# A decoder layer with product-key experts on one core: output projections split over the attention heads, expert picks turned earlier, one-hots built four tokens at a time with the gates applied by ScalarE

## The chip, the cores and the metric

One Trainium2 chip, one core, everything in float32. The metric is the device time of one launch in microseconds. The kernel is written by engine: TensorE (PE), VectorE (DVE), ScalarE (ACT), GpSimd (POOL) and SyncE (SP) each have one ordered list of instructions, tied together by counting semaphores. A matrix product in float32 shows as two entries each of weight load and matmul in the profile.

## What is computed

512 tokens (4 blocks of 128) of width 1024 go through one layer:

```
h   = x @ w_in                                   # 7 column groups of 512
r   = swish(g) * GroupNorm(retention(rot(q), rot(k), v))       # 4 heads
d   = RMSNorm((softmax(q1 k1') - lam softmax(q2 k2')) v) * 0.8 # 4 heads
x   = LayerNorm(alpha x + concat(r, d) @ w_out)
s   = (x @ w_query) . sub_keys                   # 8 heads, 2 halves, 128 keys
      top 16 of each half, top 16 of the 256 sums -> 128 experts per token
gate= softmax(best scores)
y   = sum_e gate_e * gelu(x . u_e) * v_e         # of 16384 experts
out = LayerNorm(alpha x + y)
```

## The kernel before, in words

**Two ways to the experts.** Blocks 0 and 3 are *gathered*: for each of 128 picks per token a row of 128 x 1024 is fetched by an indirect DMA (POOL, L443) into a ring of 8, `ring`; first 128 rows of u for `dot` (L1052), then 128 of v for `add_row` (L1070). That makes 512 rows, taken in a fixed order by `rows(n)`, which VectorE calls wherever its list has room. The running count is `taken[0]`. POOL issues the next gather when VectorE has used the row 8 before it. Blocks 1 and 2 are *dense*: for each of 128 expert blocks n, `up(n)` (L730) multiplies x with the block of uT, `hidden(n)` (L966) takes the Gelu, `mask_hidden(n)` (L1335) multiplies with the gates G, and `add(n, d)` (L760) sums h times the block of V in PSUM. `up(n)` may run two blocks ahead of `hidden`. Up to NH = 56 hidden blocks are kept before the main loop starts.

**The gates G** come from picks. `norm_picks(d)` (L1313) normalises their gates after ScalarE's Exp in `take_picks(d)` (L977), TensorE turns the three columns (first key, second key, gate) in `turn_picks(d)` (L740), ScalarE copies them to `pT`. `hot_quads(d)` (L1322) builds for each token two one-hots of 128, `b_hot` and `a_hot`, the second already times the gate; `quad(q)` (L749) multiplies those of four tokens, `take_quad(q)` (L985) copies the result to a stage, and every 8 quads ScalarE spills a stage of 2 MB to the buffer gd in HBM. `load_g` (L364) brings it back by expert. There are 32 quads for each of the two dense blocks d; the rings are 4 one-hot slots and 5 PSUM banks.

**Order of the work.** (1) Block 0 goes through projections, attention, output and query alone. (2) `project_1` does the projections of blocks 1 to 3 with retention between them; VectorE takes 2 rows before each rotary and 4 before each swish gate. (3) For b = 1 to 3: `attend(b)` runs four heads. For each the score of the next head, two Exps with row sums on ScalarE (`attention`, L891), `softmax_join` on VectorE, transposes, a copy and the product with v; VectorE takes 2 rows per head. `diff_norm(b)` (L1224) follows, then `mixed_out(b)` (L661): transposes, copies by ScalarE, and both halves of the output projection (`out_half`, L682) into banks W 2 and 3, in which attention also works. `attend(b+1)` waits until `ln1(b)` (L1235) has read them. (4) `query` for three blocks, with scores copied to SBUF; VectorE retrieves block 1 (`retrieve`, L1246: best_keys, best_pairs, best_experts for two heads at a time). (5) TensorE does 40 expert blocks (UP_FIRST), then picks and quads of d = 0 with one `up` per four quads, then those of d = 1. In ScalarE's list `take_picks(0)` stands behind `hidden(39)`. VectorE's list has best_keys(2, 0), norm_picks(0), the rest of that retrieve, hot_quads(0), three retrieves with three rows each, norm_picks(1), the rest of 128 dots, hot_quads(1), weigh(0). (6) The main loop of 128 steps n: TensorE `add(n)` for both d and `up(n + 56)`, VectorE `mask_hidden(n + 8)`, in the early steps the four retrieves of block 3, and 4 rows a step up to 384 rows, later 3 a step from n = 66 on, where `weigh(1)` stands. `gathered_gelu` (L958) on ScalarE waits for the last 8 dots of its block. (7) The last sums and norms.

SP loads in list order: weights as slots come free (`load_w`; the query's first weights wait for the first half of block 3's output projection), uT into 4 slots, V into 4 slots (each block when `add` has freed one), G in groups of 8.

Two orders that a sentence tells badly, VectorE's and ScalarE's lists in stage 5:

```
best_keys(2, 0); norm_picks(0); best_pairs(); best_experts(2, 0)
hot_quads(0)                                   # VectorE
for s in range(1, 4): retrieve(2, s); rows(3)
norm_picks(1); rows(E - taken[0]); hot_quads(1); weigh(0)

for n in range(UP_FIRST): hidden(n)            # ScalarE
for d in range(ND):
    take_picks(d)
    for q in range(d * QUADS, (d + 1) * QUADS):
        take_quad(q)
        if q % 4 == 3: hidden(UP_FIRST + q // 4)
gathered_gelu(0)
```

## Time and profile before

| | |
|---|---|
| median of 3 runs | 1799.67 us (1797.59 to 1803.29) |
| the profiled execution | 1803.09 us, its span 1801.0 us |
| TensorE busy | 1457.8 us (81%), mean granted clock 0.901 |
| VectorE busy | 1201.1 us (67%) |
| ScalarE busy | 174.5 us (10%) |
| GpSimd busy (issuing gathers) | 598.8 us (33%) |
| moved by DMA | 503.05 MB, mean 279 GB/s |

Busy shares are means over stages with different limits, so the table says little by itself. A group of instructions is named by its line, its engine, and what it writes and reads. A granted clock of 1.00 is TensorE's full 2.4 GHz, 0.50 the lower level of 1.2 GHz. A window's row gives, for a stretch of the span, busy time of each engine with its count in brackets (PE, PEld, DVE, ACT, POOL), then PE's granted clock, the busy share of the DMA engines and GB/s. The chain that ended last is followed back from the last instruction; each of its rows is a stretch in which that work held the end.

### The profile page before, as it was taken

Reading aid. Unit: us, or ns where it says so; the run is one execution under the profiler, and the core shown is the slowest. Engines: PE = TensorE matmul, PEld = TensorE weight load, DVE = VectorE, ACT = ScalarE, POOL = GpSimd, SP = SyncE. Lnnn points to the kernel's source line nnn. Section 1 sums busy time; section 2 is a strip of 40 time slices with the busy share of each in tenths; the row PEclk is TensorE's granted clock in tenths of the full one; section 3 lists DMA queues with packets and bytes.
Section 4 is the critical chain, followed back from the end, with each engine's and each line's share of the span. In section 5 each row is a group of like instructions: output and inputs, shape, how many; then the busy total and the mean of one; then the engine's idle time right before and its main releaser. Section 6 shows DMA issues by size and latency. Waiting matters only on the chain.

```text
span 1801.0 us, 15732 instructions
## 1 busy us (share of the span) xinstructions
PE 1457.8 (81%) x5374; PEld 937.7 (52%) x5374; DVE 1201.1 (67%) x2884; ACT 174.5 (10%) x400; POOL 598.8 (33%) x517
## 2 busy tenths in 40 slices
PE   7889998665799997930589999998988957888776
PEld 5474464333457886830475666555655535333232
DVE  2367865668478102998977998666666669776773
ACT  1110001122011111310230001000000000000000
POOL 0005131224411000004303446455455557654620
PEclk9989999666899999975698999999999978999888
DMA  9938464334933543444769999999999999999973
GB/s 344 362 130 308 174 217 147 122 117 128 354 129 101 187 153 117 152 164 157 286 222 364 365 365 359 409 405 405 408 406 404 406 408 378 405 406 405 405 294 105
DMA packets 161950, 503.05 MB, mean 279 GB/s; under 512 B 15056, under 2 KB 33744, under 8 KB 160720
## 3 DMA queue, kind: packets, MB, share of 16 engines
q0 software_dynamic: 73728, 268.47, 39.4%
q1 hardware_dynamic: 86992, 216.81, 32.7%
q10 hardware_dynamic: 1152, 16.78, 2.5%
q8 instruction: 43, 0.70, 0.2%
q14 instruction: 35, 0.29, 0.0%
HBM read 483.13 MB, written 18.87 MB: 279 GB/s over the span
## 4 chain that ended last, share of the span: by engine, by line
PE 35%; DVE 24%; DMA 24%; POOL 7%; issue 6%; SPq 1%; ACT 1%; DVEq 0%; POOLq 0%
DMA arena<-uv,idx 21%; PE X L736 9%; POOL arena L443 7%; PE W L716 6%; PE W L483 6%; DVE xs L1070 5%; DVE arena L1052 3%; PE W L763 3%; PE W L688 2%; PE W L489 2%; DVE lng L1331 2%; PE W L756 1%; DVE arena L1330 1%; DMA arena<-uv 1%; DMA arena<-w_in 1%
## 5 line engine op out<-in xcount | busy, mean ns | idle before, releaser
L443 POOL DMA_INDIRECT arena<-uv,idx x512 | 598.4, 1169 | 1126.3 <-DVE arena L1052 632.2
L736 PE MATMUL X<-arena 128*128 128x256 f32 x2048 | 458.6, 380 | 27.0 <-ACT arena L975 26.3
L736 PEld LDWEIGHTS X<-arena 128*128 128x128 f32 x2048 | 389.1, 191 | 111.6 <-issue 61.9
L763 PE MATMUL W<-arena 128*128 128x512 f32 x768 | 363.2, 625 | 62.9 <-DMA arena<-uv 52.8
L1070 DVE SCALAR_TENSOR_TENSOR xs<-arena,gate,xs 128x1024 f32<-128x1024 f32 x256 | 328.7, 1284 | 110.9 <-DMA arena<-uv,idx 98.3
L1052 DVE SCALAR_TENSOR_TENSOR arena<-arena,xs 128x1024 f32<-128x1024 f32 x256 | 306.7, 1223 | 95.5 <-DMA arena<-uv,idx 92.7
L763 PEld LDWEIGHTS W<-arena 128*128 128x128 f32 x768 | 152.6, 201 | 240.8 <-issue 205.1
L483 PE MATMUL W<-arena 128*128 128x512 f32 x320 | 143.7, 605 | 9.6 <-DMA arena<-w_in 8.9
L716 PE MATMUL W<-arena 128*128 128x128 f32 (+1 forms) x512 | 117.1, 392 | 1.4 <-ACT arena L926 1.4
L1331 DVE TENSOR_SCALAR lng<-iota_f,both_uses 128x128 f32<-128x128 f32 x256 | 106.6, 431 | 0.0
L483 PEld LDWEIGHTS W<-arena 128*128 128x128 f32 x320 | 60.8, 194 | 81.7 <-issue 77.0
L716 PEld LDWEIGHTS W<-arena 128*128 128x128 f32 x512 | 80.4, 199 | 36.3 <-issue 2.4
L756 PE MATMUL W<-lng,arena 128*128 128x128 f32 x416 | 56.6, 292 | 52.4 <-issue 40.3
L1330 DVE TENSOR_SCALAR arena<-iota_f,both_uses 128x128 f32<-128x128 f32 x256 | 94.5, 370 | 0.0
L975 ACT ACTIVATE arena<-X 128x256 f32<-128x256 f32 x96 | 36.5, 383 | 499.9 <-PE X L736 470.8
L756 PEld LDWEIGHTS W<-lng,arena 128*128 128x128 f32 x416 | 53.6, 203 | 55.3 <-issue 40.7
L763 PE MATMUL W<-arena,kT 128*128 128x512 f32 x128 | 63.1, 644 | 21.7 <-DMA arena<-uv 14.2
L1317 DVE TENSOR_REDUCE gsum<-both_uses 128x8 f32<-128x128 f32 x2 | 0.6, 284 | 118.3 <-ACT both_uses L980 118.3
L763 PE MATMUL W<-arena,rv 128*128 128x512 f32 x128 | 58.4, 608 | 14.8 <-DMA arena<-uv 11.9
L489 PE MATMUL W<-arena 128*128 128x128 f32 (+1 forms) x256 | 59.1, 389 | 5.2 <-DVE arena L1145 3.7
L763 PEld LDWEIGHTS W<-arena,kT 128*128 128x128 f32 x128 | 25.8, 206 | 54.6 <-issue 39.5
L489 PEld LDWEIGHTS W<-arena 128*128 128x128 f32 x256 | 39.1, 194 | 22.8 <-issue 6.3
(185 smaller groups left out, 971.3 us busy)
## 6 DMA issues: line engine op xcount, KB each, us to landing
arena<-uT SPq DMA_DIRECT2D x128, 512.0 KB
arena<-uv SPq DMA_DIRECT2D x128, 512.0 KB
arena<-w_in SPq DMA_DIRECT2D x13, 2048.0 KB, 13.0
arena<-peer_w_query SPq DMA_DIRECT2D x8, 2048.0 KB, 12.0
gd<-arena ACTq DMA_DIRECT2D x8, 2048.0 KB, 7.2
arena<-gd SPq DMA_DIRECT2D x16, 1024.0 KB
arena<-w_out SPq DMA_DIRECT2D x4, 2048.0 KB, 14.0
arena<-uv,idx POOLq DMA_INDIRECT x512
```

What stands on the lines that cost most here:

```text
L443: pool.indirect_dma_start(out=ring[:, s % RING, :], out_offset=None, in_=rows, in_offset=bass.IndirectOffsetOnAxis(ap=idx[:, col:col + 1], ...
L483: last = nc.tensor.matmul(bank, actT[:, k, part * P:(part + 1) * P], wts[slot][:, k, :], start=(k == 0), stop=(k == KD - 1))
L489: last = nc.tensor.matmul(bank[:, at:at + n_tok], wts[slot][:, k, h * P:(h + 1) * P], actT[:, k, toks], start=(k == 0), stop=(k == KD - 1))
L716: last = nc.tensor.matmul(dst, wts[slot][:, k, i * P:(i + 1) * P], actT[:, k, toks], start=(k == 0), stop=(k == KD - 1))
L736: last = nc.tensor.matmul(h_bank(n), u_ring[n % UR][:, k, :], actT[:, k, P:P + TD], start=(k == 0), stop=(k == KD - 1))
L756: last = nc.tensor.matmul(bank[:, m * P:(m + 1) * P], b_hot[:, q % OH_RING, m, :], a_hot[:, q % OH_RING, m, :], start=True, stop=True)
L763: last = nc.tensor.matmul(sum_banks(d)[:, half, :], h_slot(n)[:, d * P:(d + 1) * P], v_ring[n % VR][:, half * HW:(half + 1) * HW], start=( ...
L975: nc.scalar.activation(h_slot(n), h_bank(n), ACT.Gelu).then_inc(h_ready, 1)
L1052: STT(out=ring[:, r, :], in0=ring[:, r, :], scalar=1.0, in1=xs[:, GATHERED[g], :], op0=ALU.mult, op1=ALU.mult, accum_out=hid[:, col:col + ...
L1070: STT(out=xs[:, b, :], in0=ring[:, r, :], scalar=gate[:, g * E + e:g * E + e + 1], in1=xs[:, b, :], op0=ALU.mult, op1=ALU.add).then_inc(ro ...
L1330: TS(b_hot[:, q % OH_RING, m, :], iota_f[:], pT[d % 2][:, 1, t:t + 1], None, ALU.is_equal)
L1331: last = TS(a_hot[:, q % OH_RING, m, :], iota_f[:], pT[d % 2][:, 0, t:t + 1], pT[d % 2][:, 2, t:t + 1], ALU.is_equal, ALU.mult)
```

## The change

1. *Output projection.* The halves of block b's projection no longer follow `attend(b)` but stand between the heads of `attend(b + 1)`: the turn of the mixed rows beside head 0, one half beside head 1, one beside head 2, and `turn_x1(1)` beside head 3 of block 3. They use the PSUM tensors X and ACC, not W. Scores of the next block's first head are made beside the last head. VectorE's `ln1(b - 1)` moves from behind head 0 to the end of block b.
2. *Picks.* `UP_FIRST` goes; 6 expert blocks stand before the first `turn_picks`, 18 before the second, and one `up` follows every second quad. `gathered_gelu(0)` moves between the two sets of quads, `weigh(0)` in front of `hot_quads(1)`.
3. *One-hots.* One comparison of 128 x 512 for each of `b_hot` and `a_hot` instead of four of 128 x 128; `a_hot` without the gate. ScalarE scales it in place, four Copies of 128 x 128 with a column of `pT` as the scale (`gate_hot`), one quad ahead of the quad's copy.
4. *Rows.* Taken 3 and 5 in the projections (2 and 4), 2 before each retention norm (1), 1 per head (2), 6 and 24 around ln1(3) (8 and 12), 4 per retrieve of block 1 (3), 1 per two quads (0), none per retrieve of block 2 (3). By the start of the main loop 144 rows are taken instead of 128, `weigh(1)` stands at n = 62 instead of 66.

```diff
 GT = 8
-UP_FIRST = NH - ND * QUADS // 4
+UP_BEFORE = [6, 18]
+FIRST_V3 = 62
...
-        def out_banks(ph):
+        def mix_bank(b, half):
-            return [W[:, 2 * ph + half, :] for half in range(2)]
+            return X[:, half * HW:(half + 1) * HW] if b else W[:, half, :]
+        x1_bank = mix_bank
+        def out_of(b):
+            return ACC[:] if b else W[:, 2:4, :].rearrange("p a n -> p (a n)")
...
                 keys_n = (b + 1) * P
-                if h:
-                    pe.wait_ge(exps_ready, H * b + h)
-                elif b > 1:
-                    pe.wait_ge(mix_taken, 2 * b)
-                else:
+                if b == 1 and h == 0:
                     pe.wait_ge(proj_taken_act, takes(fill[0], "act"))
+                else:
+                    pe.wait_ge(exps_ready, H * b + h)
                 for c in range(2):
...
                         score(b, h + 1)
+                    elif b < NB - 1:
+                        score(b + 1, 0)
+                    beside(b, h)
                     n = H * b + h
                     pe.wait_ge(a_ready, n + 1)
-                    if b == 1 and h == 0:
-                        pe.wait_ge(ret_normed, NB)
-                    elif h == 0:
-                        pe.wait_ge(out_read, b)
+                    if h == 0:
+                        if b == 1:
+                            pe.wait_ge(ret_normed, NB)
+                        pe.wait_ge(mix_ready, b)
                     else:
...
-            def mixed_out(b):
+            def beside(b, h):
-                turn_mixed(b)
-                if b > 1:
-                    turn_x1(b - 1, out_banks(1))
-                if b < NB - 1:
-                    score(b + 1, 0)
-                if b > 1:
-                    pe.wait_ge(x1_taken, 2 * b)
-                for half in range(2):
-                    out_half(b, half)
+                if b > 1 and h == 0:
+                    turn_mixed(b - 1)
+                elif b > 1 and h < 3:
+                    out_half(b - 1, h - 1)
+                elif b == 3 and h == 3:
+                    turn_x1(1)
...
                 pe.wait_ge(mix_ready, b + 1)
+                if b == 3:
+                    pe.wait_ge(x1_taken, 4)
                 for half in range(2):
...
                         src = swish[:, b - 1, :] if half == 0 else work[:, HW:2 * HW]
-                        last = nc.tensor.transpose(W[:, half, k * P:(k + 1) * P], src[:, k * P:(k + 1) * P], ident[:])
+                        last = nc.tensor.transpose(mix_bank(b, half)[:, k * P:(k + 1) * P], src[:, k * P:(k + 1) * P],
+                                                   ident[:])
                     last.then_inc(mix_turned, 1)
...
                 pe.wait_ge(mix_taken, 2 * (b + 1))
+                if b > 1:
+                    pe.wait_ge(out_read, b)
                 slot, count = wslot(1, WIN + half)
...
                 for k in range(KD):
-                    last = nc.tensor.matmul(W[:, 2 + half, :], mixT[:, k, :], wts[slot][:, k, :],
+                    last = nc.tensor.matmul(ACC[:, half * HW:(half + 1) * HW], mixT[:, k, :], wts[slot][:, k, :],
                                             start=(k == 0), stop=(k == KD - 1))
...
                 attend(b)
-                mixed_out(b)
-            turn_x1(3, out_banks(0))
+            turn_mixed(3)
+            out_half(3, 0)
+            out_half(3, 1)
+            turn_x1(2)
+            turn_x1(3)
             query(1, WAVES[1])
             pe.wait_ge(scores_stored, 4 + 3 * WQ)
-            for n in range(UP_FIRST):
-                up(n)
+            n = 0
             for d in range(ND):
+                for _ in range(UP_BEFORE[d]):
+                    up(n)
+                    n += 1
                 turn_picks(d)
...
                     quad(q)
-                    if q % 4 == 3:
-                        up(UP_FIRST + q // 4)
+                    if q % 2:
+                        up(n)
+                        n += 1
             pe.wait_ge(quad_taken, ND * QUADS)
...
                     act.wait_ge(a_turned, n)
+                    if h == 0:
+                        act.wait_ge(squares_ready, b)
                     for c in range(2):
...
                     last.then_inc(exps_ready, 1)
+                    beside(b, h)
                     act.wait_ge(a_turned, n + 1)
...
+            def beside(b, h):
+                if b > 1 and h == 0:
+                    take_mixed(b - 1)
+                elif b == 3 and h == 3:
+                    take_x1(1)
             def take_mixed(b):
...
+            def gate_hot(q):
+                d, t = q // QUADS, 4 * (q % QUADS)
+                act.wait_ge(hot_found, q + 1)
+                for m in range(4):
+                    last = nc.scalar.activation(a_hot[:, q % OH_RING, m, :], a_hot[:, q % OH_RING, m, :], ACT.Copy,
+                                                scale=pT[d][:, 2, t + m:t + m + 1])
+                last.then_inc(hot_ready, 1)
             def take_quad(q):
...
                 attention(b)
-                take_mixed(b)
-                if b > 1:
-                    take_x1(b - 1, out_banks(1))
-            take_x1(3, out_banks(0))
+            take_mixed(3)
+            take_x1(2)
+            take_x1(3)
             query(1, WAVES[1])
-            for n in range(UP_FIRST):
-                hidden(n)
+            n = 0
             for d in range(ND):
+                for _ in range(UP_BEFORE[d]):
+                    hidden(n)
+                    n += 1
                 take_picks(d)
+                act.wait_ge(pT_ready, d + 1)
+                gate_hot(d * QUADS)
                 for q in range(d * QUADS, (d + 1) * QUADS):
+                    if q + 1 < (d + 1) * QUADS:
+                        gate_hot(q + 1)
                     take_quad(q)
-                    if q % 4 == 3:
-                        hidden(UP_FIRST + q // 4)
-            gathered_gelu(0)
+                    if q % 2:
+                        hidden(n)
+                        n += 1
+                if d == 0:
+                    gathered_gelu(0)
             for n in range(NH, NT):
...
                     gate_exp(1)
-                elif n == NH + 64:
+                elif n == NH + FIRST_V3 - 2:
                     gathered_gelu(1)
...
                 dve.wait_ge(mixer_ready, 2 * (b + 1))
-                src = W[:, 2:4, :].rearrange("p a n -> p (a n)")
-                STT(out=xs[:, b, :], in0=xs[:, b, :], scalar=ALPHA, in1=src, op0=ALU.mult,
+                STT(out=xs[:, b, :], in0=xs[:, b, :], scalar=ALPHA, in1=out_of(b), op0=ALU.mult,
                     op1=ALU.add).then_inc(out_read, 1)
...
                    op=ALU.mult).then_inc(pk_ready, 1)
+                dve.wait_ge(pk_ready, d + 1)
...
                         dve.wait_ge(quad_ready, q - OH_RING + 1)
-                    for m in range(4):
-                        t = 4 * (q % QUADS) + m
-                        TS(b_hot[:, q % OH_RING, m, :], iota_f[:], pT[d % 2][:, 1, t:t + 1], None, ALU.is_equal)
-                        last = TS(a_hot[:, q % OH_RING, m, :], iota_f[:], pT[d % 2][:, 0, t:t + 1],
-                                  pT[d % 2][:, 2, t:t + 1], ALU.is_equal, ALU.mult)
-                    last.then_inc(hot_ready, 1)
+                    t = 4 * (q % QUADS)
+                    TT(out=b_hot[:, q % OH_RING, :, :], in0=iota_f[:].unsqueeze(1).to_broadcast([P, 4, P]),
+                       in1=pT[d % 2][:, 1, t:t + 4].unsqueeze(2).to_broadcast([P, 4, P]), op=ALU.is_equal)
+                    TT(out=a_hot[:, q % OH_RING, :, :], in0=iota_f[:].unsqueeze(1).to_broadcast([P, 4, P]),
+                       in1=pT[d % 2][:, 0, t:t + 4].unsqueeze(2).to_broadcast([P, 4, P]),
+                       op=ALU.is_equal).then_inc(hot_found, 1)
+                    if q % 2:
+                        rows(1)
...
                 if FILLS[n][1] == RG:
-                    rows(4)
+                    rows(5)
                     swish_gate(n)
                 else:
-                    rows(2)
+                    rows(3)
                     rotary(n)
...
                         rows(1)
-                rows(1)
+                rows(2)
                 retention_norm(b)
...
                         softmax_max(b, h)
-                    rows(2)
+                    rows(1)
                     softmax_join(b, h)
-                    if b > 1 and h == 0:
-                        ln1(b - 1)
-                rows(2)
-                diff_norm(b)
                 if b < NB - 1:
                     softmax_max(b + 1, 0)
-            rows(8)
+                if b > 1:
+                    ln1(b - 1)
+                else:
+                    rows(2)
+                diff_norm(b)
+            rows(6)
             ln1(3)
-            rows(12)
+            rows(24)
             for s in range(4):
                 retrieve(1, s)
-                rows(3)
+                rows(4)
             best_keys(2, 0)
...
                 retrieve(2, s)
-                rows(3)
-            norm_picks(1)
             rows(E - taken[0])
-            hot_quads(1)
+            norm_picks(1)
             weigh(0)
+            hot_quads(1)
             for n in range(LEAD):
...
                         best_experts(3, s)
-                if taken[0] == 3 * E and n < 66:
-                    pass
-                else:
-                    if n == 66:
-                        weigh(1)
-                    rows(min(4, 3 * E - taken[0]) if n < 66 else 3)
+                if n == FIRST_V3:
+                    weigh(1)
+                rows(min(4, 3 * E - taken[0]) if n < FIRST_V3 else 3)
                 if n == 40:
```

Left out are new semaphore names, the matching changes of the copies on ScalarE (`take_mixed`, `take_x1` with the new banks) and the calls of `turn_x1` without a bank argument.

## Rows read from the trace of the kernel before

**Rows 1.** Windows of the kernel: busy us (x count) per engine, clock, DMA share, GB/s.

```profile
305.00:468.00 163.00, 97.78 (x301) 52.98 (x300) 113.36 (x267) 31.83 (x98) 52.42 (x39) 0.70 0.48 158
362.00:380.00 18.00, 10.13 (x33) 6.12 (x34) 17.37 (x36) 5.17 (x15) 8.86 (x7) 0.50 0.51 156
778.00:875.00 97.00, 5.79 (x30) 4.49 (x29) 86.90 (x253) 3.73 (x7) 40.92 (x34) 0.55 0.55 189
959.00:1107.00 148.00, 148.00 (x514) 97.23 (x513) 140.37 (x322) 11.19 (x25) 72.40 (x58) 1.00 0.96 357
1107.00:1495.00 388.00, 330.16 (x1081) 209.23 (x1079) 263.19 (x388) 16.48 (x43) 212.50 (x194) 0.93 1.03 405
```

**Rows 2.** The chain that ended last: start us, us, what.

```profile
224.99 4.58 DVE arena L1052 x8
...
338.21 14.99 PE W L688 x32
...
391.21 14.09 PE W L688 x32
...
468.26 23.45 PE W L716 x64
...
568.65 138.41 PE X L736 x640
...
930.45 3.80 PE W L756 x32
...
1729.49 39.72 PE W L763 x88
```

**Rows 3.** The waits: engine and line waited for, total us, times, longest.

```profile
DVE gsum L1317 <- ACT both_uses L980: 118.3, 1, 118.3
```

**Rows 4.** DMA issues on the page: line, count, KB each.

```profile
arena<-uv SPq DMA_DIRECT2D x128, 512.0 KB
```

**Rows 5.** Timeline of the attention blocks, 353 to 386 us, all engines.

```profile
353.29 1.22 DVE L1240 SCALAR_TENSOR_TENSOR xs<-xs,W 128x1024 f32<-128x1024 f32 x1 [9.43 <-PE W L688]
...
359.74 1.28 DVE L1103 SCALAR_TENSOR_TENSOR xs<-xs,lnr,lng 128x1024 f32<-128x1024 f32 x1
...
366.60 0.90 PE L653 MATMUL W<-ident,arena 128*128 128x128 f32 x3 [1.06 <-DVE arena L1203]
...
369.65 1.65 PE L635 MATMUL W<-dkT,arena 64*128 64x384 f32 x4
...
381.96 0.17 DVE L1228 TENSOR_SCALAR rstd<-ssq 128x4 f32<-128x4 f32 x1 [2.10 <-ACT arena L910]
...
384.35 1.13 DVE L1231 SCALAR_TENSOR_TENSOR arena<-W,rstd,both_uses 128x128 f32<-128x128 f32 x4
```

**Rows 6.** Timeline of DVE from 560 to 820 us.

```profile
566.78 0.87 DVE L1257 MAX8 best_v<-rv 128x8 f32<-128x128 f32 x4 [5.21 <-ACT rv L949]
...
720.24 0.28 DVE L1330 TENSOR_SCALAR arena<-iota_f,both_uses 128x128 f32<-128x128 f32 x1
...
777.69 0.53 DVE L1331 TENSOR_SCALAR lng<-iota_f,both_uses 128x128 f32<-128x128 f32 x1
...
797.05 0.87 DVE L1257 MAX8 best_v<-kT 128x8 f32<-128x128 f32 x4
...
812.54 1.22 DVE L1052 SCALAR_TENSOR_TENSOR arena<-arena,xs 128x1024 f32<-128x1024 f32 x1
```

**Rows 7.** Groups of instructions by form: busy us, mean ns, idle before.

```profile
L1297 DVE TENSOR_TENSOR cand<-pos_f,iota_f 128x512 f32<-128x512 f32 x32 | 22.3, 697 | 1.1
...
L975 ACT ACTIVATE arena<-X 128x256 f32<-128x256 f32 x96 | 36.5, 383 | 499.9 <-PE X L736 470.8 <-issue 29.1
...
L991 ACT ACTIVATE arena<-W 128x512 f32<-128x512 f32 x52 | 31.0, 597 | 77.4 <-PE W L756 77.4
...
L975 ACT ACT_TABLE_LOAD x4 | 5.1, 1283 | 0.1
...
L871 ACT ACTIVATE arena<-X,nmax 128x128 f32<-128x128 f32 x8 | 2.8, 376 | 9.0 <-DVE nmax L1212 9.0
```

25 lines of the change are left out of this document (14 added, 11 removed).

## The prediction

> **What bounds the kernel now.** I read the windows first, stage by stage, then the waits, the chain that ended last, and the two timelines where a stage is neither full of matrix work nor of transfers. The last 850 us are held by transfers: from 1107 us until the gathers end the DMA engines are busy all the time, at 405 GB/s up to 1495 us [rows 1]. Between 959 and 1107 us TensorE (148 of 148 us) and VectorE (140) are full too, at 357 GB/s. Only the tail is TensorE's: 88 matrix entries in 39.7 us, 0.451 us each, and one step n has 8 of them, so 3.6 us a step [rows 2].
>
> Before that the engines take turns. For 118.3 us VectorE stands in front of norm_picks(0), because ScalarE takes the Exp of the picks only after 40 expert blocks [rows 3], and the 40 blocks are 138.4 us of TensorE, 3.46 us each [rows 2]. Then VectorE alone works from 778 to 875 us (86.9 of 97 us) with TensorE at 5.8 us [rows 1]. In attention neither is full: 97.8 and 113.4 of 163 us [rows 1]; TensorE does both halves of an output projection in 14.99 and 14.09 us [rows 2] in front of the next block's transposes.
>
> So two things decide the end: when the main loop can start, and how many rows of 512 KB [rows 4] are still to be gathered by then.
>
> **Projections.** Nine rows more are taken there. A row is 4.58/4 = 1.15 us of VectorE [rows 2]. VectorE has slack except in front of the second and third swish gate, where the row of the chain at 225 us stands; one of the added rows lies on it: **+1.2 us**. The others are covered by VectorE's waits for TensorE, and would cost 1.15 us each without them (bounds 0 and 10).
>
> **Attention** now takes 163 us [rows 1]. I walk it with the present durations. A row fewer per head and one fewer at the end of block 1 leave the first block 23.0 instead of 27.3 us. In block 2 head 0 needs a row, a join and the maxima and Exp of head 1: 5.8 us. Heads 1 and 2 each hold half a projection, 7.0 us (half of 14.09 [rows 2]), between the score of the next head and the transposes. From transposes to the next score it is 369.65 - 366.60 = 3.05 us, the score is 1.65 [rows 5]: 11.6 us a head, where VectorE has nothing to hide the half with, since its next maxima and join hang on the Exp behind it. Then join, the maxima of block 3 (4.4), ln1 of block 1 (353.29 to 361.02, 7.7) and the norm (381.96 to 385.48, 3.5, with its mark 3.6) [rows 5]: 5.8+23.2+4.4+7.7+3.6 = 44.7. Block 3 has longer rows: 6.5+2 x 12.7+1.9+7.7+3.6 = 45.1, with turn_x1(1) beside it. Last come transposes and copies (2.7), both halves of block 3 (14.0), ln1 (7.7), transposes and copies (2.7): 27.1. Sum 23.0+44.7+45.1+27.1 = 139.9 from the first maxima at 306.5, so the query would start at 446.4 instead of 468: -21.6 us. SP's queue: the query's first weights, 2 MB, wait for the first half of block 3 and then have 17 us, at 0.405 MB/us 5.2 us alone, so they stay hidden; so do POOL's gathers, eight deep in the ring. **The clock** takes something back. In the heads the granted clock is 0.50, the lower level of 1.2 GHz [rows 1], and of the present projections the first, after a longer stretch of such work, took 0.9 us more than the second (14.99 and 14.09 [rows 2]). Four halves will start behind small work where two pairs did; I take 0.5 us each, near that row: **-19.5 us**. Bounds: -25 (no such cost, and copies that overlap) and -8 (0.9 us at each of six pieces, and 8 us of joins that come late). The Trainium skill, "TensorE: Matmul & The Clock Gate", section on the HAM clock gate, says that the array gets every pulse only after it was kept busy and half of them after idling. By that rule, applied to each half, the part would be rival (b); the trace has both levels, 0.50 here and 1.00 in the early main loop [rows 1], and no row of halves that stand alone.
>
> **From the query to the first one-hot.** The query itself is unchanged, 568.65 - 468.26 = 100.4 us [rows 2], and starts at 468.3+1.2-19.5 = 450.0; the first block of uT at 550.4, the sixth ends at 571.2. VectorE's 24 rows after ln1(3) run into the loads of the query's weights; four more of them would still be covered, as block 1's last scores come 566.78 - 468.26 = 98.5 us into the query [rows 6], at 548.5. From there retrieve 812.54 - 797.05 = 15.5 us, four rows 4.6, and best_keys to best_experts with norm_picks between them 16.4: 585.0. One-hots are two 128x512 comparisons; the nearest row is L1297, a comparison with both inputs broadcast, 0.697 us [rows 7]. That is 1.3 us a quad against 57.9/32 = 1.8 now (720.24 to 778.2) [rows 6]. First matmul of a quad at about 587.6. TensorE, that had been at it until 709 us, idles 16 us here.
>
> **A set of 32 quads** is now 57.9 us, bound by VectorE. After the change TensorE has 16 blocks between the 32 quads. Four quads are 3.80 us [rows 2], so two are 1.8 and with the block 3.46+1.8 = 5.26 us a pair. VectorE needs 2 x 1.3+1.15 = 3.8 and is no bound. ScalarE has eight scalings, two quad copies of 0.60 and one Gelu of 0.38 [rows 7]. A scaling of 128x128 by a column: 0.376 us is the nearest row, an Exp with such an operand (L871); plain forms take 0.383 for 256 columns and 0.597 for 512, so by their slope 0.276 for 128 [rows 7]. Four in a row are 1.1 to 1.5 us, and I take 1.3. Sum 2.6+1.2+0.4 = 4.2: no bound either. But it is in order: behind an odd quad ScalarE waits for the block, does Gelu (0.38), and only then scales the second next quad (1.3), while TensorE has one quad ready (0.9). **Added wait:** 0.8 us a pair, bounds 0.3 and 1.1; behind it queue the quad and the block after it. A pair is 6.04, a set 96.6 us, 1.5 us more for the cold start: 587.6 to 685.7.
>
> **Between the sets.** VectorE is free some 9 us before, at 677, and does three retrieves (46.5) and the last nine dots (10.3): 733.8. gathered_gelu(0) stands in ScalarE's queue in front of hidden(22), so TensorE gets two blocks ahead and then waits for that very moment. The 18 blocks of UP_BEFORE thus do not run beside VectorE: 16 x 3.46 = 55.4 us, and 2.5 for the clock, end at 792.5, with VectorE waiting, as in [rows 3], for the Exp (table load 1.28 [rows 7], 1.9 in all). Norm (0.9), weigh(0) (some 2.1, five short instructions) and the first one-hot and scaling (2.6) give 800.0. The second set ends at 897.1 with its block (0.5 for the clock), its last quad at 893.6; now that is 930.45+3.80 = 934.2 [rows 2]. **The main loop starts 40.6 us earlier**; less the 18.3 of the two parts above, **22.3 us** come from here (bounds 10 and 38, by the two ends of the wait and 4 us of DVE's lead).
>
> **Main loop.** 144 rows instead of 128 are taken by then, so the first two thirds take 60 steps, not 64, and gathers end at step 104, not 108. Before that point 16 gathers and 4 blocks of V fewer must land: 20 x 0.524 MB at 0.405 MB/us [rows 1, 4] is -25.9 us. But the four steps are then in TensorE's tail, 4 x 3.6 = +14.4 [rows 2]. Sum: **-11.5 us**. Bounds -5 and -20 (the early steps, which TensorE and VectorE fill, give nothing back or everything).
>
> **Sum.** +1.2 - 19.5 - 22.3 - 11.5 = -52.1 against 1803.1 us for the profiled execution (span 1801.0): 1751.0. That execution lies 3.4 us above the median of the three runs, 1799.7, from which the same sum gives 1747.6. I say 1748. The measurement can tell about 0.3%, 5.4 us, from nothing.
>
> **Rivals.**
> (a) *The wait in the quads is hidden and the halves cost less*: ScalarE at its lower prices leaves 0.3 us a pair (-16), attention gives its 25 (-5): 1727. For it, ScalarE's 4.2 of 5.3 us; against it, its order.
> (b) *Half clock in attention*: all six halves at 1.2 GHz, 14 us instead of 7: +42, 1790. For it the 0.50 among the heads, against it the 14.09 us of a present pair, behind heads at 0.50 [rows 1, 2].
> (c) *The early rows return nothing*, since TensorE (148 of 148) and not DMA sets the early main loop: 1760.
> (d) *Table loads, slower than before*: each pair has a scaled copy behind a Gelu. If the scaled form needs another table, that is two loads of 1.28 us a pair on the in-order wait, 32 x 2.56 = 82 us: 1830. It decides from 52/32 = 1.6 us a pair. Against it: plain copies and Gelus alternate now with 4 loads in all [rows 7].
> (e) *The early turn does not come about*, VectorE waits for something else in the first set as long as now: the middle gives 0, 1770.
>
> **Chances.** Forecast 0.62, (a) 0.11, (b) 0.05, (c) 0.10, (d) 0.03, (e) 0.09. The forecast alone spans 1735 to 1762. The range reaches to (a) and (e), 1726 to 1770. Slower is 0.04, (d) and 0.01 for (b) with the bad ends of the other bounds; within 0.3% 0.02, from (b) too; faster 0.94.
>
> **What would show it.** In the waits, VectorE's 118 us gone and a wait of some 55 to 60 us in front of the second norm_picks; TensorE idle some 16 us before the first quad and 40 us behind the 24th block; the last quad at 894 us; a quad pair at 6.0 us; query at 450; the last gathered row added 66 us earlier than now, with 17 steps of tail behind it. The step that is weakest is the attention walk: half projections of 7 us at 1.00 confirm it, 14 us refute it. Wrong would also be a first set shorter than 85 us, or a main loop whose DMA share falls below 1.0 after its first 150 us.

## The result, and the profile after

| | before | after |
|---|---|---|
| median (range), 4 runs each | 1800.89 us (1797.59 to 1803.29) | 1741.39 us (1738.73 to 1744.23) |
| profiled execution, its span | 1803.09, 1801.0 us | 1741.73, 1739.7 us |
| VectorE busy | 1201.1 us | 1163.3 us |
| ScalarE busy | 174.5 us | 241.9 us |

The ratio is 0.9671, with a 95% interval of 0.9648 to 0.9694. The changed kernel takes 61.3 us less by the spans of the two profiled executions (59.5 by the medians), where the prediction's sum was 52.1. Below, "the set" is the 32 quads of one dense block, and "a block" of TensorE is one expert block of `up`, 16 matrix entries.

The stages come out of four marks on the chain: the first attention score (305.73 before, 309.34 after), the query's first matmul, the last spill of the second set (`gd<-arena`, the eighth of eight), and the end. The third mark of the kernel before:

```profile
934.90 7.15 DMA gd<-arena
```

| stretch | before | after | change | forecast |
|---|---|---|---|---|
| start to first attention score | 305.7 | 309.3 | +3.6 | +1.2 |
| attention, to the query | 162.5 | 135.6 | -27.0 | -19.5 |
| query to the last spill | 466.6 | 447.5 | -19.2 | -22.3 |
| last spill to the end | 866.1 | 847.3 | -18.8 | -11.5 |

The chain that ended last, after; start us, us, what:

```profile
226.28 5.72 DVE arena L1097 x10
232.75 8.25 PE W L497 x16
...
340.18 7.44 PE ACC L699 x16
350.58 7.06 PE ACC L699 x16
382.38 7.06 PE ACC L699 x16
...
418.04 16.38 PE ACC L699 x32
444.89 23.51 PE W L729 x64
...
582.62 3.78 PE W L769 x16
...
716.76 10.32 DVE arena L1097 x18
727.83 58.28 PE X L749 x256
793.71 3.78 PE W L769 x16
...
892.35 7.13 DMA gd<-arena
```

The pairs of halves of 14.99 and 14.09 us [rows 2] are now four separate halves; the pair of block 3 is still a pair. The query has come forward from 468.26 to 444.89. The 640 entries in one piece in front of the quads [rows 2] are gone, and in their place stand 256 entries at 727.83, behind the last dots.

The waits of after; engine and line waited for, total us, times, longest:

```profile
PE X L749 <- ACT arena L1004: 67.2, 2, 37.1
...
DVE gsum L1361 <- ACT both_uses L1009: 61.1, 1, 61.1
```

VectorE's 118.3 us [rows 3] have become 61.1 in front of the other norm_picks. ScalarE's timeline has the Gelu of the gathered block, `gathered_gelu(0)`, with its wait in brackets:

```profile
727.10 0.31 ACT L993 ACTIVATE hid<-hid 128x128 f32<-128x128 f32 x1 [42.89 <-DVE arena L1097]
```

The three waits lock one another: ScalarE waits 42.9 us for the last dots, TensorE 37.1 for ScalarE to take the Gelu of block 22, and then VectorE 61.1 for ScalarE to come to the Exp behind the blocks.

Windows of after (columns as in rows 1): the first set, the dots without blocks, the blocks without dots, and most of the main loop:

```profile
583.00:676.00 93.00, 82.58 (x474) 73.83 (x474) 61.67 (x125) 55.78 (x164) 15.37 (x16) 0.98 0.69 237
676.00:728.00 52.00, 14.13 (x73) 12.20 (x72) 49.25 (x166) 3.86 (x11) 8.58 (x5) 0.69 0.35 113
728.00:792.00 64.00, 58.65 (x259) 50.64 (x259) 3.56 (x10) 8.23 (x19) 3.75 (x4) 0.95 0.52 180
...
1069.00:1430.00 361.00, 301.83 (x987) 192.09 (x986) 246.06 (x380) 15.84 (x42) 198.95 (x181) 0.92 1.03 405
```

Read the second and third together. VectorE is busy 49.25 of 52 us while TensorE has 14.13, and then TensorE 58.65 of 64 us while VectorE has 3.56. Those are two pieces of work that need nothing of each other, one behind the other. In the first set no engine is full: TensorE 82.58 of 93 us, VectorE 61.67, ScalarE 55.78. The main loop is bound by transfers as before, 405 GB/s [rows 1].

One pair of quads on the chain inside the first set:

```profile
599.10 3.47 PE X L749 x16
...
602.59 0.38 ACT arena L1004
602.97 1.17 ACT lng L1019 x4
...
604.19 1.16 PE W L769 x8
605.35 3.47 PE X L749 x16
```

From one block to the next it is 6.25 us. TensorE ends the block, ScalarE takes its Gelu, then scales the next quad, and only then has TensorE something to do. The scaling, and the table loads on the line of that Gelu (busy us, mean ns, idle before):

```profile
L1019 ACT ACTIVATE lng<-lng,both_uses 128x128 f32<-128x128 f32 x256 | 80.9, 391 | 12.4 <-DVE lng L1376 12.4
...
L1004 ACT ACT_TABLE_LOAD x4 | 5.1, 1283 | 0.1
```

Table loads have stayed at 4 on the line of the blocks' Gelu, as in [rows 7], and the scalings' own line has none. The new comparison of 128 x 512 takes VectorE 690 ns.

### The profile page after: what moved, and what is told of

It is laid out like the page before. It is cut to its first block, busy times and chain, and to the rows that moved or that the text cites. A ratio compares the mean times of both kernels' runs of the same rounds, so it can differ in the third digit from the quotient of the medians.

```text
span 1739.7 us, 15609 instructions
## 1 busy us (share of the span) xinstructions
PE 1458.6 (84%) x5374; PEld 936.8 (54%) x5374; DVE 1163.3 (67%) x2500; ACT 241.9 (14%) x656; POOL 589.1 (34%) x517
## 3 DMA queue, kind: packets, MB, share of 16 engines
q0 software_dynamic: 73728, 268.47, 41.3%
## 4 chain that ended last, share of the span: by engine, by line
PE 46%; DVE 21%; DMA 20%; POOL 4%; ACT 4%; issue 3%; SPq 2%; DVEq 0%; ACTq 0%
DMA arena<-uv,idx 13%; PE X L749 11%; PE W L776 11%; PE W L729 7%; PE W L491 6%; DMA arena<-uv 5%; POOL arena L451 4%; DVE xs L1115 4%; DVE arena L1097 3%; PE ACC L699 3%; PE W L497 2%; ACT lng L1019 2%; PE W L769 2%; DMA arena<-w_in 1%; PE W L739 1%
## 5 line engine op out<-in xcount | busy, mean ns | idle before, releaser
L451 POOL DMA_INDIRECT arena<-uv,idx x512 | 588.6, 1150 | 1064.5 <-DVE arena L1097 490.7
L749 PE MATMUL X<-arena 128*128 128x256 f32 x2048 | 465.3, 382 | 67.9 <-ACT arena L1004 67.2
L776 PE MATMUL W<-arena 128*128 128x512 f32 x768 | 356.1, 615 | 51.1 <-DMA arena<-uv 39.5
L491 PE MATMUL W<-arena 128*128 128x512 f32 x320 | 144.0, 606 | 10.5 <-DMA arena<-w_in 9.8
L769 PE MATMUL W<-lng,arena 128*128 128x128 f32 x416 | 60.7, 293 | 34.0 <-ACT lng L1019 34.0
L1374 DVE TENSOR_TENSOR arena<-iota_f,both_uses 128x512 f32<-128x512 f32 x64 | 44.2, 690 | 61.9 <-PE W L769 48.9
L1019 ACT ACTIVATE lng<-lng,both_uses 128x128 f32<-128x128 f32 x256 | 80.9, 391 | 12.4 <-DVE lng L1376 12.4
L769 PEld LDWEIGHTS W<-lng,arena 128*128 128x128 f32 x416 | 55.4, 202 | 40.5 <-ACT lng L1019 39.2
L1389 DVE TENSOR_TENSOR arena<-arena 128x256 f32<-128x256 f32 x96 | 38.3, 418 | 30.1 <-DMA arena<-gd 30.1
```

The lines of the kernel that those rows point to most:

```text
L451: pool.indirect_dma_start(out=ring[:, s % RING, :], out_offset=None, in_=rows, in_offset=bass.IndirectOffsetOnAxis(ap=idx[:, col:col + 1], ...
L491: last = nc.tensor.matmul(bank, actT[:, k, part * P:(part + 1) * P], wts[slot][:, k, :], start=(k == 0), stop=(k == KD - 1))
L749: last = nc.tensor.matmul(h_bank(n), u_ring[n % UR][:, k, :], actT[:, k, P:P + TD], start=(k == 0), stop=(k == KD - 1))
L769: last = nc.tensor.matmul(bank[:, m * P:(m + 1) * P], b_hot[:, q % OH_RING, m, :], a_hot[:, q % OH_RING, m, :], start=True, stop=True)
L776: last = nc.tensor.matmul(sum_banks(d)[:, half, :], h_slot(n)[:, d * P:(d + 1) * P], v_ring[n % VR][:, half * HW:(half + 1) * HW], start=( ...
L1019: last = nc.scalar.activation(a_hot[:, q % OH_RING, m, :], a_hot[:, q % OH_RING, m, :], ACT.Copy, scale=pT[d][:, 2, t + m:t + m + 1])
```

## The experiments

Twelve kernels. Those from the changed kernel first ask where its remaining loss sits and what its one-hots are worth (1 to 4), then what its parts gave (5, 6, and 12 from the kernel before), then how far the cure goes (7 to 11). The kernel before ran at 1801.5 to 1802.3 us beside them, and all ratios are against it.

| | kernel | us (range) | ratio, 95% interval |
|---|---|---|---|
| 1 | Gelu of the gathered block behind the 18 blocks | 1702.29 (1700.46 to 1703.86) | 0.9449 [0.9434, 0.9465] |
| 2 | 24 blocks first, none between the sets | 1744.31 (1741.74 to 1748.80) | 0.9683 [0.9661, 0.9705] |
| 3 | one-hots and gates on VectorE as before | 1713.23 (1711.35 to 1715.63) | 0.9512 [0.9496, 0.9527] |
| 4 | ScalarE scales one quad further ahead | 1713.57 (1713.18 to 1716.31) | 0.9514 [0.9498, 0.9530] |
| 5 | kernel before, with split projections alone | 1789.64 (1787.87 to 1791.44) | 0.9926 [0.9903, 0.9950] |
| 6 | no rows added in the second set | 1758.24 (1757.33 to 1761.77) | 0.9762 [0.9737, 0.9787] |
| 7 | 1 and 4 | 1672.01 (1670.60 to 1674.43) | 0.9281 [0.9257, 0.9304] |
| 8 | 7 with 10 blocks first | 1673.43 (1672.10 to 1676.27) | 0.9288 [0.9265, 0.9312] |
| 9 | 7 with 9 blocks first, norm later | 1665.10 (1661.12 to 1668.76) | 0.9241 [0.9217, 0.9265] |
| 10 | 9 with 8 more rows in the second set | 1658.41 (1654.32 to 1660.45) | 0.9201 [0.9178, 0.9225] |
| 11 | 1 and 3 | 1670.86 (1668.75 to 1672.62) | 0.9274 [0.9251, 0.9297] |
| 12 | kernel before, with early turn alone | 1752.22 (1746.12 to 1753.74) | 0.9719 [0.9694, 0.9744] |

### 1. The Gelu of the gathered block, behind the 18 blocks

```diff
@@ ScalarE's list, for d in range(ND)
                 for _ in range(UP_BEFORE[d]):
                     hidden(n)
                     n += 1
+                if d:
+                    gathered_gelu(0)
                 take_picks(d)
...
-                if d == 0:
-                    gathered_gelu(0)
```

> Changed kernel, with gathered_gelu(0) behind the 18 expert blocks in ScalarE's list instead of in front of them. Theory (two queues take turns): the 18 blocks now run while VectorE does its three retrieves and nine dots. They end 18 x 3.46 = 62 us after the first set of quads, at about 745 us instead of 786, and the second set starts at about 753 instead of 793.7: 41 us less, total 1741 - 41 = 1700 (1697 to 1706), and ScalarE's hold of TensorE (PE X waits for ACT, 37 us) is gone. Rival (the main loop is what counts, being held by DMA, and an earlier start is partly given back): the second set starts 41 us earlier but the total falls by 20 or less, 1720 or more.

39 us less than the changed kernel, and the second set starts at 753.35 instead of 793.71. The chain of this kernel:

```profile
679.89 65.63 PE X L749 x304
```

The blocks now follow the first set without a hole, beside VectorE's dots, and the wait in front of the second norm_picks has shrunk from 61.1 to

```profile
DVE gsum L1361 <- ACT both_uses L1009: 21.2, 1, 21.2
```

The edit moves one short ScalarE instruction past 18 blocks that don't need it, and nothing else.

### 2. All blocks in front of the first quads

```diff
-UP_BEFORE = [6, 18]
+UP_BEFORE = [24, 0]
```

> Changed kernel with UP_BEFORE = [24, 0] instead of [6, 18]: the picks of the first dense block turn 18 expert blocks later, none stand between the sets. Theory (the serial wait between the sets takes back what the early turn gives): first quad 62 us later, at about 644, first set ends about 744, VectorE's retrieves and dots at about 792, and the second set starts at once behind them, at about 799: 6 us later than now, total about 1747 (1742 to 1752). Rival (the early turn is what made the change faster): the 62 us are lost, 1795 or more.

1744.31 us, 3 more than the changed kernel, which the intervals of the two don't tell from nothing. The first quad is 60 us later (643.10 against 582.62), the second set starts at 794.87 against 793.71. VectorE waits the same 62 us, at the first norm_picks instead of the second:

```profile
DVE gsum L1361 <- ACT both_uses L1009: 63.9, 2, 61.9
```

With ScalarE's list as the change has it, turning the picks 18 blocks earlier thus gives almost nothing: 62 us of cover won in front are lost behind. The run doesn't undo the early turn as a whole, though: its first quad still comes 79 us before that of the kernel before (643.10 against 722.18), since 24 blocks stand in front instead of 40. A changed kernel with 40 in front was not run.

### 3. One-hots and gates on VectorE, as before

```diff
-                    TT(out=b_hot[:, q % OH_RING, :, :], in0=iota_f[:].unsqueeze(1).to_broadcast([P, 4, P]),
...
+                    for m in range(4):
+                        t = 4 * (q % QUADS) + m
+                        TS(b_hot[:, q % OH_RING, m, :], iota_f[:], pT[d % 2][:, 1, t:t + 1], None, ALU.is_equal)
+                        last = TS(a_hot[:, q % OH_RING, m, :], iota_f[:], pT[d % 2][:, 0, t:t + 1],
+                                  pT[d % 2][:, 2, t:t + 1], ALU.is_equal, ALU.mult)
+                    last.then_inc(hot_found, 1)
...
-                pe.wait_ge(hot_ready, q + 1)
+                pe.wait_ge(hot_found, q + 1)
```

The `gate_hot` calls of ScalarE's list are gone with it.

> Changed kernel with the one-hots of the kernel before: eight comparisons of 128x128 a quad on VectorE, the gate in the second one, and no scaling on ScalarE. Theory (a pair of quads is 6.25 us only because TensorE waits for ScalarE's scaling; its own work is 5.26): VectorE needs 8 x 0.45 + 1.15 = 4.8 us a pair, still less than TensorE, so a pair falls to 5.3 us, each set by 15 us, total about 1741 - 31 = 1710 (1706 to 1718). Rival (the cheaper one-hots are what made the sets fit): VectorE becomes the bound, a pair takes 6.2 us or more, total 1741 or more.

28 us less than the changed kernel. A window of its first set:

```profile
580.00:660.00 80.00, 80.00 (x482) 73.68 (x481) 78.19 (x305) 24.94 (x46) 15.56 (x16) 0.98 0.77 276
```

TensorE is full, 80.00 of 80 us, at 5.24 us a pair. VectorE is nearly so, 78.19 us, and that costs nothing. Added to the other parts, the third part of the change made the kernel slower by 28 us.

### 4. ScalarE scales a quad ahead

```diff
-                    if q + 1 < (d + 1) * QUADS:
+                    end = (d + 1) * QUADS
+                    if (q % 2 or q == d * QUADS) and q + 1 < end:
                         gate_hot(q + 1)
+                    if q % 2 and q + 2 < end:
+                        gate_hot(q + 2)
```

> Changed kernel, ScalarE scales one quad further ahead: behind an odd quad it scales the quad after the next before it waits for the expert block. Theory (the wait is one of order in ScalarE's list, not of its load of 4.5 us a pair): the waits of TensorE for the scaled rows vanish, a pair falls from 6.25 to 5.3 us, total about 1710 (1706 to 1716), the same as with the gates on VectorE. Rival (ScalarE is loaded too high and only the bound moves): a pair stays above 5.9 us, total 1733 or more.

1713.57 us. The chain inside its first set has no ScalarE left, only TensorE, 1.78 + 3.46 = 5.24 us a pair:

```profile
605.03 0.89 PE W L769 x8
605.92 0.89 PE ACC L769 x8
606.81 3.46 PE X L749 x16
```

The one-hots with ScalarE's scaling cost as much as those of VectorE alone, within 0.4 us, once the scaling doesn't stand behind the wait for a block. The 28 us were the order of ScalarE's list, not its work: the window 583 to 676 us has ScalarE at 60.14 us here and 55.78 in the changed kernel.

### 5. Split projections alone, from the kernel before

`attend` calls what stands beside each head, as in the change; picks, rows, quads and one-hots stay as before.

```diff
-            def mixed_out(b):
+            def beside(b, h):
-                turn_mixed(b)
-                if b > 1:
-                    turn_x1(b - 1, out_banks(1))
-                if b < NB - 1:
-                    score(b + 1, 0)
...
+                if b > 1 and h == 0:
+                    turn_mixed(b - 1)
+                elif b > 1 and h < 3:
+                    out_half(b - 1, h - 1)
+                elif b == 3 and h == 3:
+                    turn_x1(1)
```

> Kernel before with the attention part alone: halves of the projection between the heads of the next block, ln1 at the block's end, and everything else (rows taken, picks, one-hots, main loop) as before. In the changed kernel the stretch from the first attention score to the query's first matmul is 27 us shorter, but it also takes 16 rows fewer there. Theory (rows are exposed except beside a half): the 4 heads of block 1, heads 0 and 3 of blocks 2 and 3 and the rows at the ends of blocks 2 and 3 bring back some 12 rows of 1.15 us, so the split itself is worth 13 us: total about 1788 (1784 to 1792). Rival (the rows are hidden and the split does it all): 27 us, 1775 or less.

12.7 us less than the kernel before. The chain:

```profile
341.57 7.67 PE ACC L699 x16
...
425.62 16.92 PE ACC L699 x32
453.00 23.79 PE W L729 x64
```

From the first score (304.70) to the query it is 148.3 us, 14.2 less than before. The change has 135.6. In this stretch the two kernels differ only in the rows that VectorE takes, so the other 12.7 of the 27.0 come from those.

### 6. No rows added in the second set

```diff
-FIRST_V3 = 62
+FIRST_V3 = 66
...
-                    if q % 2:
+                    if q % 2 and d == 0:
```

> Changed kernel without the 16 added rows in the second set of quads, so that the main loop begins with 128 rows taken and weigh(1) stands at n = 66, as before. From the last quad on this is the kernel before. Theory (all of the main loop's gain is these 16 rows): the second set takes as long as now, and the total rises by the 18.8 us by which the stretch behind the last quad became shorter: about 1760 (1757 to 1763). Rival (my sum of 11.5 was right and 7 us came from elsewhere): 1753 or less.

17 us more than the changed kernel. The second set and its last spill keep their times (792.34 and 890.99, against 793.71 and 892.35), so all of it is main loop. VectorE's timeline of the kernel before at the first adds of the main loop and at `weigh(1)`:

```profile
957.78 2.68 DVE L1070 SCALAR_TENSOR_TENSOR xs<-arena,gate,xs 128x1024 f32<-128x1024 f32 x2
...
1499.21 2.71 DVE L1070 SCALAR_TENSOR_TENSOR xs<-arena,gate,xs 128x1024 f32<-128x1024 f32 x2
```

541.4 us between the two, and 541.5 in this run (912.70 to 1454.18). In the changed kernel, with the end of its last gathered row:

```profile
914.15 5.44 DVE L1115 SCALAR_TENSOR_TENSOR xs<-arena,gate,xs 128x1024 f32<-128x1024 f32 x4
...
1424.29 4.07 DVE L1115 SCALAR_TENSOR_TENSOR xs<-arena,gate,xs 128x1024 f32<-128x1024 f32 x3
...
1667.02 5.11 DVE L1389 TENSOR_TENSOR arena<-arena 128x256 f32<-128x256 f32 x15
```

510.1 us (914.15 to 1424.29). The 16 rows take four steps out of this phase: 16 gathers, 4 blocks of V and 4 of U, 24 x 0.524 MB at 0.405 MB/us = 31.1 us, and 31.3 are measured.

### 7. Both cures

The edits of 1 and 4 together.

> Changed kernel with gathered_gelu(0) behind the 18 blocks and ScalarE's scaling one quad further ahead, both together. Theory (TensorE is then the bound from the first quad to the last): the two gains of 39 and 28 us add up, since VectorE's dots (at about 712) still end before the 18 blocks (at about 730): total about 1674 (1670 to 1680). Rival (the faster sets only expose VectorE, or the main loop gives the start back): 1690 or more.

1672.01 us, 69.4 less than the changed kernel, against 39.1 + 27.8 = 66.9 for the two alone. The two losses sat in different stretches (the hole between the sets, the pairs within them), and so they add.

### 8. Ten blocks first

```diff
-UP_BEFORE = [6, 18]
+UP_BEFORE = [10, 14]
```

> The kernel with both mends and UP_BEFORE = [10, 14]: four of the blocks that stood between the sets go in front of the first picks, where TensorE idles some 14 us until VectorE has the first one-hot. Theory: the first quad is held by VectorE and stays where it is, the second set starts 14 us earlier; 1660 (1657 to 1665) if the kernel with both mends gives 1674. Rival (the Exp of the picks comes 14 us later in ScalarE's list and holds norm_picks and the first quad back by as much): no gain, within 3 us of that kernel.

No gain (1673.43). The theory was that TensorE idles in front of the first quad and could do four blocks there for nothing. The chain says that the idle time had moved, not gone:

```profile
545.20 34.81 PE X L749 x160
...
580.44 1.28 ACT L1009
...
596.01 3.78 PE W L769 x16
```

Ten blocks end at 580.0, the Exp stands behind their Gelus, and VectorE, which waits 13.6 us for it, still has best_pairs and best_experts to do: 14.3 us between the end of the Exp's table load (the piece of 1.28 us) and the first quad. Counted from the query's first matmul (444.74, in 7 442.64), the first quad is 13.6 us later than in 7, against 4 x 3.46 = 13.8 us of blocks won, and the second set starts after 293.6 us where 7 has 293.8. That is the rival.

### 9. Nine blocks first, and norm_picks(0) behind best_experts

```diff
-UP_BEFORE = [6, 18]
+UP_BEFORE = [9, 15]
...
-            norm_picks(0)
             best_pairs()
             best_experts(2, 0)
+            norm_picks(0)
```

> The kernel with both mends, UP_BEFORE = [9, 15], and norm_picks(0) moved behind best_experts(2, 0), so that the Exp of the picks may come 10 us later. With ten blocks first and norm_picks in its old place the first quad was 11 us later, because the Exp stands behind the blocks in ScalarE's list. Theory (that list is the whole cause): the Exp ends at about 579, when VectorE is ready for it, the first quad comes 2 us later than with six blocks, three blocks of 3.46 us are gone between the sets: 8 us less than the kernel with both mends, about 1664 (1661 to 1668). Rival (TensorE is the bound in any order, moving blocks gives nothing): within 3 us of 1672.

1665.10 us, 6.9 less than 7. The steps must be counted from the query, because this execution already starts it 4.2 us later, with nothing changed up to there. The query's first matmuls in 7 and in this run:

```profile
442.64 23.51 PE W L729 x64
```

```profile
446.86 23.66 PE W L729 x64
```

From there the first quad comes after 139.4 us (586.23), in 7 after 137.7 (580.36): 1.7 later, where 2 were expected. The second set comes after 286.1 us (732.92), in 7 after 293.8 (736.40): 7.7 earlier, where 8 were expected. So the theory holds in its steps too. (Its "11 us later" for ten blocks is 13.6 by the same count.)

### 10. More rows in the second set

```diff
-FIRST_V3 = 62
+FIRST_V3 = 60
...
-                    if q % 2:
+                    if q % 2 or d and q % 4 == 2:
```

> The kernel of e9_nine_first with 24 instead of 16 added rows in the second set of quads (three in four quads), 152 rows taken before the main loop, weigh(1) at n = 60. Theory (16 rows taken early are worth 17 us, and VectorE and the DMA engines still have room in the set, 9.4 us of work in 10.5 a four of quads and some 350 of 405 GB/s): 8 more rows give 8.5 us, about 1656 (1652 to 1660). Rival (the gathers no longer come in time and the set grows): 1662 or more.

1658.41 us, 6.7 less than 9, the fastest of all: 83 us below the changed kernel and 143 below the one before. Its window between the two sets:

```profile
669.00:728.00 59.00, 55.80 (x260) 48.69 (x258) 48.65 (x164) 8.57 (x20) 12.31 (x9) 1.00 0.69 238
```

Between the sets TensorE (55.80) and VectorE (48.65 of 59 us) now work side by side, where the changed kernel needs 52 + 64 us one after the other. The second set takes eight more rows and isn't longer (its last spill starts at 816.46, in 9 at 817.23), but the rows give 6.7 us where 8.5 were expected.

### 11. One-hots on VectorE, Gelu late

The edits of 1 and 3 together.

> Changed kernel with the one-hots of the kernel before (gates on VectorE) and gathered_gelu(0) behind the 18 blocks. Theory (cheaper one-hots are worth nothing while TensorE bounds the sets): the same 1672 to 1675 as with ScalarE's scaling ahead. Rival (VectorE, later free, now ends its dots behind the 18 blocks, and the cheaper one-hots begin to count): 1680 or more.

1670.86 us against 1672.01 for 7: the same within the intervals. With TensorE the bound of a pair, the new one-hots are worth nothing by time. What they leave is room on VectorE, which 10 uses for its eight rows; whether the old ones would have had that room beside 78.19 of 80 us was not run.

### 12. The early turn alone, from the kernel before

```diff
-UP_FIRST = NH - ND * QUADS // 4
+UP_BEFORE = [6, 34]
...
-            for n in range(UP_FIRST):
-                up(n)
+            n = 0
             for d in range(ND):
+                for _ in range(UP_BEFORE[d]):
+                    up(n)
+                    n += 1
```

and the same in ScalarE's list, with one block per four quads as before and `gathered_gelu(0)` at its old place at the end.

> Kernel before with the early turn alone: 6 expert blocks before the first picks, 34 between the sets (with one per four quads as before, 56 in all). gathered_gelu(0), weigh(0), rows, one-hots and attention stay as before. Theory (the early turn is worth most where nothing serial takes it back, and here gathered_gelu(0) stands behind both sets): the first quad comes at about 604 us instead of 722, the 34 blocks run while VectorE retrieves, norm_picks(1) is held by their Exp until about 785, then 26 dots in 40 us, and the second set starts at about 825 instead of 875: 50 us less, total about 1752 (1747 to 1757). Rival (TensorE and VectorE swap turns, the 118 us of waiting only move): less than 20 us, 1782 or more.

1752.22 us: this part by itself takes 49.3 us off the kernel before. TensorE's timeline shows the first set early, at 603.79 us:

```profile
603.79 6.59 PE L756 MATMUL W<-lng,arena 128*128 128x128 f32 x32 [11.27 <-DVE lng L1337]
```

The second set starts at 825.77. In this kernel 34 blocks stand behind the first set, and the order of ScalarE's Gelu doesn't hold them up. They run beside VectorE's retrieves, and VectorE then waits 67.4 us for the Exp behind them, before its last dots. This and run 2 belong together: turning after 6 blocks instead of 40 is worth about 50 us here, where the blocks behind it run beside VectorE's work, and turning after 6 instead of 24 is worth at most 3 us in the changed kernel, where `gathered_gelu(0)` holds them.

## Why the prediction was right, and where not

**The whole.** 1741.4 us against a forecast of 1748, in the range of 1726 to 1770, and faster as said. The likeliest case is the one that came: each wait that it named is there. Two sizes were off by more than 5 us, attention and the main loop, both with more gain than forecast (7.5 and 7.3); projections and the middle gave 2.4 and 3.1 less, so the total is nearer than its parts.

**Projections, +1.2, measured +3.6.** The row on the way to the swish gate cost its 1.15 us (5.72 instead of 4.58). This execution's first matmuls start 1.1 us later for no reason of the change. The rest was not foreseen: TensorE's 16 entries behind that wait took 8.25 us, where the same ones of the kernel before took 7.09. Their granted clock was 0.65 against 0.76. The longer wait in front (TensorE idle 4.86 us instead of 3.71) doesn't explain it: of the eleven executions with the same five rows there, eight have 8.17 to 8.37 us for these entries, but runs 9, 10 and 11 have 7.04, 6.83 and 6.85. Run 9:

```profile
234.04 7.04 PE W L497 x16
...
340.32 8.50 PE ACC L699 x16
```

In those three the first half of attention takes 8.4 to 8.5 us, in the other eight 7.4 to 7.5. What decides it stays open. The other eight rows were covered, as said.

**Attention, -19.5, measured -27.0.** Here the term was mis-sized, by the walk (-21.6) and by its clock term (+2). TensorE's timeline of the changed kernel around the first half:

```profile
338.53 1.65 PE L641 MATMUL W<-dkT,arena 64*128 64x384 f32 x4
340.11 7.51 PE L699 MATMUL ACC<-arena 128*128 128x512 f32 x16
347.47 0.49 PE L662 MATMUL W<-ident,arena 128*128 128x128 f32 x3
348.54 0.94 PE L666 MATMUL W<-arena 128*128 128x128 f32 x6 [0.58 <-ACT arena L924]
349.66 0.92 PE L641 MATMUL W<-dkT,arena 64*128 64x384 f32 x4 [0.19 <-ACT arena L919]
```

Windows of the small work in front of that half and behind it:

```profile
335.48:340.10 4.62, 4.04 (x13) 2.35 (x13) 3.96 (x9) 1.75 (x6) 0.94 (x1) 0.50 0.43 118
347.47:350.40 2.93, 2.16 (x14) 1.29 (x12) 0.69 (x3) 1.62 (x5) 0.00 (x0) 1.00 0.00 0
```

The first half, behind small work at the low clock, took 7.44 us by the chain; the next took 7.06, and both halves of block 2 too. More than that, the small work behind a half ran at the high clock (granted 1.00, in front of the half 0.50): transposes 0.49 us where the walk had 0.90, the product with v 0.94 for 1.65, a score 0.92 for 1.65. From one half to the next it is 10.4 and 10.7 us instead of 11.6. From the transposes of one block's result to those of the next it is 41.2 and 41.3 us (332.90, 374.10, 415.38) where the walk had 44.7 and 45.1. The term for the clock had the wrong sign: with a long product in it, a head has its small work at the high clock too. The trace of the kernel before could have told this, for the small work right behind its first pair is as fast:

```profile
353.11 0.92 PE L635 MATMUL W<-dkT,arena 64*128 64x384 f32 x4
354.66 0.53 PE L653 MATMUL W<-ident,arena 128*128 128x128 f32 x3 [0.63 <-DVE xs L1240]
```

The walk took its prices from the next head, 366.60 and 369.65 [rows 5], 0.90 and 1.65. Only the last pair lost, 16.38 instead of 14.0 us, with TensorE idle 7.7 us before its transposes; the walk's last piece was 27.1 and took 29.5. Run 5 gives 14.2 us of the 27.0 to the split with the order it brings, and 12.7 to the rows moved away. The prediction had folded both into one walk. The Trainium skill's page "TensorE: Matmul & The Clock Gate", section on the HAM clock gate, says that the array gets every clock pulse once it was kept busy. The 0.49 us transposes behind a half, at a granted clock of 1.00, agree, and rival (b), which read the same rule as 14 us for each half, is refuted by 7.06.

**Query to first quad.** 137.6 us forecast, 137.7 measured (444.89 to 582.62). The step held with all its parts.

**A pair of quads, 6.04 us, measured 6.25.** The added wait came as described: ScalarE in order behind the block, with the Gelu (0.38 us), then four scalings, 1.27 us together, forecast 1.3. The 0.2 us missing is the quad behind the scaling, 1.16 us for 8 entries instead of the 0.89 of a quad that doesn't wait (chain of 4). Over 16 pairs that is 3.4 us; the second set ran 98.0 us to its last quad, with 93.6 forecast. What the wait costs as a whole is shown by runs 3 and 4: 28 us, of which the forecast had 26 (32 pairs by 0.8). The Trainium skill's page "ScalarE: Activation LUTs" gives, in the section on what ACT_TABLE_LOAD costs, 280 ns + 0.833 ns a column for an ACTIVATE with a pointer operand, an estimate of 387 ns for 128 columns. The measured mean is 391, so the trace agrees.

**Between the sets.** Blocks from 733.8 to 792.5 were forecast, 727.83 to 786.11 came; from there to the second set 7.5 and 7.6 us. (The forecast's terms, 733.8 + 55.4 + 2.5, give 791.7; it has 0.8 us more without a term.) The waits of 37 and 61 us are those named, and run 1 shows their cause: with the Gelu moved TensorE's 37 are gone, VectorE's fall to 21, and the total by 39 us. The prediction saw this lock and priced it, but called it only a step of the sum. It was the largest loss in the change.

**Main loop, -11.5, measured -18.8.** The direction and the place were right, the size was too small by two terms. Gone by the last gathered row are 72.7 us (1739.8 to 1667.1), with 66 forecast: the first phase gave 31.3; the next phase has four more blocks of U to land and took 2.2 us more, where 5.2 lie in the forecast; the rest, 43.6, is the earlier start. The tail from the last row to the sums grew from 42.8 to 54.2, by 11.4 us and not 14.4: behind the last row the trace has 111 matrix entries of TensorE instead of 86, 25 more and not the 32 of four steps, so part of the four steps was already done by then. Run 6 has the whole of this part in one number, 17 us. That speaks against rival (c), by which it would be nothing.

**The other rivals.** (a) fell for its first half, the wait is not hidden; its second, 25 us of attention, came and was passed. (d) fell: table loads stayed at four. (e) fell: VectorE's first wait is gone. Run 2 shows how near to it the kernel stood: with 61.9 us of wait left at the old place, in front of the first norm_picks, the time is the same. As for what the title lists: alone, from the kernel before, the early turn gives 49 us (12) and the split 13 (5); taken out of the changed kernel, the added rows are worth 17 (6) and the new one-hots cost 28 (3). These don't add up to 61, since the Gelu ahead of the blocks, which came with the change, took 39 as well, and with them much of what the early turn is worth alone.

**Still open.** Why the halves behind short small work come at the high clock, where the first needs 7.4 to 8.5, was not tried by itself, and nothing was run on the 16 entries of the projections that take 8.2 us in most executions and 6.9 in some. What the moved rows in front of the query and of block 1's retrieves are worth was not run alone either.

## What to carry to other kernels

An engine's list is a queue: before moving an instruction that waits for another engine, list what stands behind it and needs nothing of it; here one Gelu ahead of 18 blocks cost 39 us and one scaling behind a block's Gelu 28, and both went away by reordering alone. When work is moved from one engine to another, look whether the first was the bound: VectorE at 78 of 80 us beside a full TensorE was no reason to relieve it, and its relief changed nothing (7 against 11). Run 10 puts eight more rows on VectorE; whether it needs the relief for them was not run. Try the parts of a change alone, since its gain of 61 us hid two losses that together were larger.

## What was not expected of the hardware

- Short matrix work gains from long matrix work among it. Transposes behind a half took 0.49 us for 3 entries (granted clock 1.00), 0.90 in front of it (0.50), and a score 0.92 instead of 1.65. The kernel before shows the same behind its pairs.
- The same work behind the same wait isn't always granted the same clock: 16 entries took 8.2 to 8.4 us in eight executions and 6.8 to 7.0 in three, and the first half of attention 7.4 to 7.5 in those eight and 8.4 to 8.5 in those three. A difference of 1 us there proves nothing about a change.
- A pair of halves, behind 7.7 us of idle time and eight transposes, took 16.38 us, and 16.92 behind 10.0 us in run 5, against 14.09 for a pair of the kernel before behind 4.8 us and more small work [rows 2].
- A quad that starts as soon as its four scalings are done takes 1.16 us instead of 0.89.
- ScalarE alternates Gelu, plain copies and copies scaled by a column with no table load between them; four scalings of 391 ns take 1.27 us, so the next starts before the last has ended.
